# Modulation weights of a fused two-block transformer: eight buffers at the front, three in the heads, columns by transposes, and VectorE's weight splits placed later

## The reference

```python
s_lat = jax.nn.silu(c)[:, None, :]
s_ctx = jax.nn.silu(c_ctx)[None, None, :]
for i in range(DEPTH):                       # DEPTH = 2
    mod_l = jnp.split(s_lat @ ada_w[i] + ada_b[i], ADA_CHUNKS, axis=-1)   # ada_w[i]: 1024 x 6144
    mod_c = jnp.split(s_ctx @ ada_w[i] + ada_b[i], ADA_CHUNKS, axis=-1)
    h_lat = rms_norm(x_lat) * (1.0 + mod_l[1]) + mod_l[0]
    h_ctx = rms_norm(x_ctx) * (1.0 + mod_c[1]) + mod_c[0]
    ...                                      # retention_mixer(h_ctx, h_lat, w_in, ...) in layer 0
```

```python
proj = x @ w_in                              # qa ka va qb kb vb and the gates gl
ya = banded_attention(qa, ka, va) @ w_branch_a
yb = weighted(dilated_attention(qb, kb, vb) in 3 groups) @ w_branch_b
ga, gb = jnp.split(sigmoid(gl + b_gate), 2, axis=-1)
h = (ga * ya + gb * yb) @ w_out
```

## Time and profile before

| | us |
|---|---|
| median of 3 runs | 2275.52 |
| lowest, highest | 2269.53, 2278.43 |
| the profiled execution | 2268.73 |
| its span | 2266.9 |
| TensorE busy in it | 2112.4 (93%) |
| VectorE busy | 1129.0 (50%) |
| ScalarE busy | 877.7 (39%) |

### The profile page before, as it was taken

The page is one execution under the profiler, slowest core; times in us unless marked ns, Lnnn a source line. Parts: engine busy times, 40 slices in busy tenths (PEclk is TensorE's granted clock), DMA queues, the critical chain, the costliest instruction groups (busy, mean ns, idle before and its releaser), DMA issues.

```text
span 2266.9 us, 27438 instructions
## 1 busy us (share of the span) xinstructions
PE 2112.4 (93%) x11538; PEld 1762.1 (78%) x11538; DVE 1129.0 (50%) x1304; ACT 877.7 (39%) x1019; POOL 47.7 (2%) x75
## 2 busy tenths in 40 slices
PE   5799999999899999999988999998899999979998
PEld 3566676676777888877768998888799988878997
DVE  2314243242523243375666454766675567557555
ACT  3332232222322213245565443653454446434442
POOL 0000000000000000000000000000000000000000
PEclk9899999999999999999999999999999999999999
DMA  6634342535255333322134654553366545335552
GB/s 214 205 117 136 105 142 81 185 113 166 56 149 170 109 103 93 106 95 85 64 85 139 187 176 163 171 175 106 130 205 193 189 160 166 128 121 186 190 195 79
DMA packets 250637, 319.57 MB, mean 141 GB/s; under 512 B 9361, under 2 KB 165298, under 8 KB 250514
## 3 DMA queue, kind: packets, MB, share of 16 engines
q1 hardware_dynamic: 236050, 263.37, 36.2%
q0 software_dynamic: 14464, 54.45, 7.1%
HBM read 316.73 MB, written 1.05 MB: 140 GB/s over the span
## 4 chain that ended last, share of the span: by engine, by line
PE 74%; DVE 11%; DMA 5%; ACT 4%; DVEq 3%; issue 2%; ACTq 1%; POOL 0%; SPq 0%; POOLq 0%
PE ps L2126 22%; PE ps L2127 21%; PE ps L2128 21%; DMA raw<-ada_w 4%; DVE w_lo L1216 3%; PE ps L2143 3%; PE ps L2154 2%; PE ps L2234 2%; ACT w_hi L587 1%; DVE big_lo L1221 1%; PE ps L2289 1%; PE ps L2173 1%; DVEq L1233 1%; DVE hT_lo L1221 1%; ACT arena L834 1%
## 5 line engine op out<-in xcount | busy, mean ns | idle before, releaser
L1216 DVE TENSOR_TENSOR w_lo<-raw,w_hi 128x2048 fp32r<-128x2048 f32 (+1 forms) x244 | 553.2, 2273 | 480.7 <-ACT w_hi L587 480.1
L587 ACT ACTIVATE w_hi<-raw 128x2048 fp32r<-128x2048 f32 (+1 forms) x244 | 461.8, 1897 | 245.2 <-PE ps L2128 229.0
L2126 PE MATMUL ps<-h_hi,w_hi 128*128 128x256 f32 x1120 | 319.2, 285 | 2.9 <-DVE h_lo L1221 2.9
L2127 PE MATMUL ps<-h_lo,w_hi 128*128 128x256 f32 x1120 | 317.5, 283 | 0.0
L2128 PE MATMUL ps<-h_hi,w_lo 128*128 128x256 f32 x1120 | 317.4, 283 | 0.0
L2126 PE MATMUL ps<-w_hi,big_hi 128*128 128x512 f32 x760 | 302.3, 398 | 14.4 <-issue 10.2
L2127 PE MATMUL ps<-w_lo,big_hi 128*128 128x512 f32 x760 | 298.3, 392 | 0.0
L2128 PE MATMUL ps<-w_hi,big_lo 128*128 128x512 f32 x760 | 297.7, 392 | 0.0
L2126 PEld LDWEIGHTS ps<-h_hi,w_hi 128*128 128x128 f32 x1120 | 215.5, 192 | 6.1 <-issue 5.3
L2127 PEld LDWEIGHTS ps<-h_lo,w_hi 128*128 128x128 f32 x1120 | 215.6, 193 | 0.8 <-issue 0.2
L2128 PEld LDWEIGHTS ps<-h_hi,w_lo 128*128 128x128 f32 x1120 | 215.5, 192 | 0.0
(11 more groups left out here) (282 smaller groups left out, 2669.7 us busy)
## 6 DMA issues: line engine op xcount, KB each, us to landing
raw<-ffn_w_in SPq DMA_DIRECT2D x88, 512.0 KB, 5.1
raw<-ada_w POOLq DMA_DIRECT2D x40, 1024.0 KB, 5.6
raw<-w_in SPq DMA_DIRECT2D x80, 512.0 KB, 4.6
raw<-w_up SPq DMA_DIRECT2D x64, 512.0 KB, 4.8
raw<-w_down SPq DMA_DIRECT2D x64, 512.0 KB, 4.5
raw<-ret_w_in SPq DMA_DIRECT2D x48, 512.0 KB, 4.7
raw<-ffn_w_out SPq DMA_DIRECT2D x40, 512.0 KB, 4.5
raw<-diff_w_in SPq DMA_DIRECT2D x24, 512.0 KB, 4.6
```

Source lines behind the costliest of these rows:

```text
L587: act.activation(SPLIT_HI[PAIR_OF[u]][:, 0:m], raw[:, RAW_OF[u], 0:m], ACT.Copy).then_inc(sem["hi_ready"], 1)
L1216: op(SPLIT_LO[PAIR_OF[u]][:, 0:m], raw[:, RAW_OF[u], 0:m], SPLIT_HI[PAIR_OF[u]][:, 0:m].bitcast(F32), ALU.subtract).then_inc(sem["lo_ready ...
L2126: pe.matmul(out, a[0], b[0], start=start, stop=False)
L2127: pe.matmul(out, a[0], b[1], start=False, stop=False)
```

## The change

**Front.** The four chunks get eight half-chunk buffers `FRONT_IN`, laid over `big_hi` and `big_lo`, which are empty then. All units are split units now, `WHOLE` and its bookkeeping go, and the order on SP's queue becomes chunk 0, chunk 2, qa0, chunk 1, chunk 3, qb0. The six small vectors are issued by ScalarE instead of SP, x and ctx come first on POOL's queue and have a semaphore each. x is squared, scaled, turned (to `XTL`, in slot 0 of `raw`) and modulated apart from ctx, and strips qa0 and qb0 are done for the two x tiles first, then for the ctx tiles, with chunks between.

**Heads.** The halves 0 to 23 go round three buffers, two front buffers and slot 0; from 24 on slot 0 alone.

**Columns.** `to_cols` turns the four 128 x 128 blocks by transposes; VectorE adds the four partial sums with a reduction, then the bias.

**Layers.** In VectorE's stream four `ahead` calls move behind other work.

```diff
-    out = [("A0", 2, UNIT, True), ("A2", 2, UNIT, True), ("qa0", 1, UNIT, False)]
-    out += [("A1", 2, UNIT, True), ("A3", 2, UNIT, True), ("qb0", 1, UNIT, False)]
+    out = []
     for h in range(RH):
+        out += [(f"{n}{h}", UNIT) for n in ("qa", "qb", "g0", "g1", "va", "vb")]
...
-        r = u % 4 if u < 8 else 1 + (u - 8) % 3
+        r = 1 + u % 3
...
+        FRONT_IN = [sb(f"front{j}", [P, 4, 512], F32, big_at + 4 * UNIT * j)[:, :, :] for j in range(8)]
+        EXTRA_IN = [FRONT_IN[3], FRONT_IN[7], raw[:, 0, :].rearrange("p (k n) -> p k n", k=4)]
+        def extra_at(e):
+            return (e % 3, e // 3 + 1) if e < 24 else (2, e - 15)
...
# SP
             modulation(0)
+            modulation(1)
+            part(w, 0, 0, RH * RDK)
             modulation(2)
-            part(w, 0, 0, RH * RDK)
-            modulation(1)
             modulation(3)
             part(w, 4, 0, RH * RDK)
...
# POOL, modulation(e)
-                if e:
-                    pool.wait_ge(sem["ada_used"], e)
-                else:
-                    pool.wait_ge(sem["unit_used"], FIRST_END["qa0"])
-                fetch(raw[:, 0, :]..., kpn(A["ada_w"][d])[...], sem["ada_in"])
+                if e == 0:
+                    pool.wait_ge(sem["front_used"], 4)
+                if e == 2:
+                    pool.wait_ge(sem["xm_ready"], 4)
+                if e >= 3:
+                    pool.wait_ge(sem["ada_used"], e - 2 if e < 24 else e)
+                fetch(EXTRA_IN[extra_at(e)[0]], kpn(A["ada_w"][d])[...], ada_in[extra_at(e)[0]])
...
# ACT, the front
+            front(1)
             row(0, 8960, 0)
             turned_x(0)
+            front(2)
+            row(1, 9472, 1)
             turned_x(1)
+            act.drain()
+            act.wait_ge(sem["mod_ready"], 2)
+            modulate(0, 0, 1, 0, 0, lambda c: XTL[:, c, :])
+            split(FIRST_END["qa0"])
+            act.wait_ge(sem["xn_ready"], 2)
             turned_x(2)
             turned_x(3)
             act.drain()
+            modulate(0, 0, 1, 1, 0, lambda c: XTC[:, c, :])
+            split(FIRST_END["qb0"])
+            front(3)
             row(0, 8960, 2)
+            front(4)
             row(1, 9472, 3)
             act.wait_ge(sem["mod_ready"], 4)
+            modulate(0, 0, 1, 0, 4, lambda c: XTL[:, c, :])
+            modulate(0, 0, 1, 1, 4, lambda c: XTC[:, c, :])
...
# DVE, mod_cols
-                op(mod[:, d, 4 * n:4 * n + 4, :], bank(b)[:, 0:8].rearrange("p (j m) -> p j m", m=2), bias, ALU.add).then_inc(sem["mod_ready"], 1)
+                parts = bank(b).rearrange("p (j q m) -> p j m q", j=4, q=4)[:, :, 0:2, :]
+                m = mod[:, d, 4 * n:4 * n + 4, :]
+                dve.tensor_reduce(m, parts, AX.X, ALU.add)
+                drain()
+                op(m, m, bias, ALU.add).then_inc(sem["mod_ready"], 1)
...
# DVE, a layer of the second program
                 maxima_b()
+                normalise_b()
                 ahead("G4")
-                normalise_b()
                 ahead("G5")
...
                 maxima_b()
-                ahead("G7")
                 normalise_b()
                 pv_lo_b(1)
+                ahead("G7")
                 used("BA0")
...
                 branch_a(3, 21)
-                ahead("BA1")
                 ... (ple_hi: one subtraction)
                 pv_lo_b(2)
+                ahead("BA1")
                 pt_lo(5, 3)
                 pv_lo_b(3)
-                ahead("PL")
...
                 mix_lo(3)
+                ahead("PL")
                 ahead("BB")
...
# PE, to_cols
-                    i = pe.matmul(bank(b)[:, 2 * j:2 * j + 2], at(a, 512)[:, j * P:(j + 1) * P], select, start=True, stop=True)
+                    i = turn(bank(b)[:, j * P:(j + 1) * P], at(a, 512)[:, j * P:(j + 1) * P])
...
# PE, the front
+            strip(4, "qa0", hT, 0, 4, range(4), True, False, (0, 1))
+            chunk(2, 0)
             pe.wait_ge(sem["mod_ready"], 2)
             to_cols(2, 8960)
+            pe.wait_ge(sem["h_part"], 2)
+            strip(4, "qa0", hT, 0, 4, (0, 1), True, False, (2, 3))
+            chunk(3, 1)
+            strip(4, "qa0", hT, 0, 4, (2,), True, False, (2, 3))
             to_cols(3, 9472)
+            used(strip(4, "qa0", hT, 0, 4, (3,), True, False, (2, 3)))
+            pe.wait_ge(sem["h_part"], 3)
+            strip(4, "qb0", hT, 4, 4, range(4), False, True, (0, 1))
             pe.wait_ge(sem["h_part"], 4)
+            used(strip(4, "qb0", hT, 4, 4, range(4), False, True, (2, 3)))
```

More of the change, by code:

```diff
@@ L118 @@
 D0, U1 = FIRST_AT["q0a"], FIRST_AT["r0"]
-def unsplit():
-    out = [False] * TOTAL_UNITS
-    for name, n, _, whole in NAMED:
-        for u in range(FIRST_AT[name], FIRST_END[name]):
-            out[u] = whole
-    return out
-WHOLE = unsplit()
-SPLIT_UNITS = [u for u in range(TOTAL_UNITS) if not WHOLE[u]]
-SPLIT_NO = [sum(not w for w in WHOLE[:u]) for u in range(TOTAL_UNITS)]
-ORDER = [name for name, _, _, whole in NAMED if not whole]
 def slots():
@@ L181, in sizes @@
     out = [UNIT] * TOTAL_UNITS
-    for name, _, m, _ in NAMED:
-        out[FIRST_END[name] - 1] = m
+    for name, m in NAMED:
+        out[FIRST_AT[name]] = m
     return out
@@ L255, in build @@
         p_read = [sem["p_read0"], sem["p_read1"]]
-        unit_in = [ctx.enter_context(nc.semaphore(f"unit_in{r}")) for r in range(RAW_SLOTS)]
+        unit_in = {r: ctx.enter_context(nc.semaphore(f"unit_in{r}")) for r in range(1, RAW_SLOTS)}
+        front_in = [ctx.enter_context(nc.semaphore(f"front_in{j}")) for j in range(8)]
+        ada_in = [ctx.enter_context(nc.semaphore(f"ada_in{j}")) for j in range(3)]
         ident = const[:, C_IDENT:C_IDENT + P]
         dist = const[:, C_DIST:C_DIST + 384]
-        select = const[:, C_SEL:C_SEL + 2]
         def at(a, *dims):
@@ L366, in load @@
                 v = RAW_BEFORE[u]
-                if v is not None and WHOLE[v]:
-                    sp.wait_ge(sem["unit_used"], v + 1)
-                elif v is not None:
-                    sp.wait_ge(sem["lo_ready"], SPLIT_NO[v] + 1)
+                if v is not None:
+                    sp.wait_ge(sem["lo_ready"], v + 1)
                 for j in range(2):
@@ L593, in ahead @@
             def ahead(name):
-                split(SPLIT_UNITS[ORDER.index(name) + 2] + 1)
+                split(FIRST_END[name] + 2)
                 act.drain()
@@ L1308, in _ @@
             rows_split(0, 0)
+            split(FIRST_END["qa0"])
             rows_split(1, 0)
-            split(FIRST_END["qa0"])
+            split(FIRST_END["qb0"])
             mod_cols(2, 0, 1)
             mod_cols(3, 0, 3)
-            split(FIRST_END["qb0"])
             rows_split(0, 4)
@@ L2155, in sums, with chunk @@
                 return i
-            def chunk(name, b):
-                for j in range(2):
-                    u = FIRST_AT[name] + j
-                    pe.wait_ge(unit_in[RAW_OF[u]], 32 * RAW_FILL[u])
-                    used(sums(b, raw[:, RAW_OF[u], :].rearrange("p (k n) -> p k n", k=4), 4 * j))
+            def chunk(j, b):
+                for h in range(2):
+                    pe.wait_ge(front_in[2 * j + h], 32)
+                    i = sums(b, FRONT_IN[2 * j + h], 4 * h)
+                i.then_inc(sem["front_used"], 1)
             def extra(b):
                 e = s.next("extra") - 1
-                pe.wait_ge(sem["ada_in"], 16 * (e + 1))
-                sums(b, raw[:, 0, :].rearrange("p (k n) -> p k n", k=4), 4 * (e % 2)).then_inc(sem["ada_used"], 1)
+                r, n = extra_at(e)
+                pe.wait_ge(ada_in[r], 16 * n)
+                sums(b, EXTRA_IN[r], 4 * (e % 2)).then_inc(sem["ada_used"], 1)
             def to_cols(b, a):
```

157 lines of the change are left out of this document (71 added, 86 removed).

## The result

| | before | after |
|---|---|---|
| median us, same chip (4 runs each) | 2276.56 (2269.53 to 2278.43) | 2209.43 (2201.62 to 2218.7) |
| ratio of times | | 0.972, interval [0.970, 0.975] |
| the profiled execution, its span | 2268.7, 2266.9 | 2218.7, 2216.9 |

The change saves 67 us, 3%. The forecast was 2193; 2209 lies in its range, 16 us above it.

The account below looks back on a forecast made before the run. TensorE, busy 93% of the span, was taken to bound the kernel. Savings of 19 + 25 + 7 + 27 = 78 us from 2268.7 gave 2191, plus 2 for the median: 2193 us, own range 2176 to 2209.

Parts of the forecast that it names:

- Term 1: Front, to the end of strip qb0: without the slot limit 19 us saved, bounds 12 and 24.
- Term 2: Heads: three buffers remove the modulation-weight waits and the low clock behind the longest; 25 us saved, bounds 16 and 26.
- Term 3: Transposes instead of selector products in 20 places outside the front: 7 us saved, bounds 5 and 8.
- buffers do not help: Rival, heads: landings stretch or POOL's order holds one back, 25 us not gained; 2218 us, chance 0.09.
- Turns dear: Rival: four transposes apart from others may cost more than a quarter of 16 in a row; 2202 us, chance 0.03.
- Term 4: Two layers: VectorE's splits moved behind urgent work, 27 us saved, bounds 12 and 34.
- (d): Layers, gate mixes: without the split ahead of them the output strip starts earlier; 3.7 us saved, 1.4 of low clock.
- (a): Layers: softmax scaling before w_lo's subtraction frees 3.3 us, but the next softmax round follows only about 2.8 earlier.
- (b): Layers, at 1554.84 us: the same reordering of scaling before w_lo's subtraction, 2.6 us more.
- (c): Layers, turn at 1576.41: short subtractions first, turn 6.5 us earlier; with two of low clock, embedded values 8.5 earlier.
- given back in the layers: Rival: moved splits come late, TensorE waits for w_lo, only about 10 of 27 us stay; 2210 us, chance 0.16.

Follow-up runs that it names:

- e1: Changed kernel with POOL's queue issuing the decay and the lambdas ahead of x and ctx: 2207.79 us, 0.9719.
- e10: Changed kernel with small transfers first, values' splits ahead of G6, G7 and BA1 and of BA1's gates, x squared before lambda's exponential: 2186.63 us.
- e8: e1 with the fetch of ctx also waiting for chunk 0 to land: 2213.61 us, 0.9737.
- e3: Changed kernel with each modulation load of the heads waiting for the use of the one before it: 2239.74 us, 0.9858.
- e11: e10 with the selector products in place of the transposes: 2195.58 us, 0.967.
- e2: Changed kernel with VectorE's four splits in the layers put back where they stood: 2231.81 us, 0.9822.
- e4: Changed kernel with the selector products in place of the transposes: 2209.08 us, 0.9739.

## Why the prediction was nearly right, step by step

**Term 1, the front, 19 us: mis-sized, about 8 came.** Strip qb0 ends at 78.4 us, not at 65.5; the forecast itself named 72 as the mark of a wrong front. The slot limit did go, and nothing there waits for a buffer. The step that failed is "ScalarE is stuck until lam's exponential at 13.72": I carried this time over from a profile in which the decay and the lambdas had their own place on the wires. The change put x and ctx, 2 MB, ahead of them on POOL's queue, and the exponential came at 21.40. Everything behind it slid: the turn of x to 26.14 (18.5 forecast), strip qa0 to 42.10 (33), strip qb0 to 64.48 (52.6). I had taken off 1 us for small vectors that "now share the wires with x on ScalarE's queue", and not looked at what stands behind x on POOL's. e1 gave back 4 us of the 7.7; e10 put the squares where they don't wait for lambda, and 1.8 more came. e8 excludes ctx's share of the wires as the cause of the rest, whose origin stays open between the vectors' new queue and the weights beside them. The forecast's chain of durations was nearly right: from the turn of x to qa0 it gave 14.5 us, and 16.0 were needed; from there to qb0 19.6, and 22.4; for qb0 12.9, and 13.9. So of the 12.9 us by which the front ends late, 7.6 are the turn's and 5.3 such small excesses.

**Term 2, the weights in the heads, 25 us: right.** With term 3's part (13 of its groups by 0.35 us, 5) the forecast asks 30 in this stretch, 29 came; e3 alone gives 27 for the buffers, in the two parts foreseen: 18.1 us of waits, and low clock. The rival "buffers do not help" has fallen.

**Term 3, the turns, 7 us: right in kind, 9 measured** (e11; 9 also by the rows). Four transposes take 0.35 us to the next start, where the forecast had 0.44, so 0.46 us a place were saved and not 0.35. The page that spoke against it, the Trainium skill's "TensorE: Matmul & The Clock Gate", Part 4, with some 275 ns a transpose, gives the wrong sum for these: the row of e10 has 0.60 us for all four from the first start to the last end, and 16 back to back take 0.11 us each. "Turns dear" has fallen.

**Term 4, the layers, 27 us: mis-sized, 9.5 to 13.6 came in the profiles, 19 to 20 by e2's and e1's medians.** Without the clock 16 us came, where the forecast's waits alone (10.2 a layer) made 20. Point (d) came as counted: the 5.1 us of the earlier trace rows became 1.3. Points (a) and (b) came for the first and third turns, which wait no more (3.4 and 2.6 before). But the second turn's wait grew from 0.5 to 3.1 us, since G6's split (2.29 us) stood ahead of 0.4 us of urgent work, the very pattern that the change undoes elsewhere; I had looked only at the splits that it moves. In (c) 3.3 of 4.1 us stayed. The clock made the larger error in the profiles: I booked 3.4 us a layer as *saved* low clock, each beside a wait that would go. None can be shown to be saved. The profiled executions had 29 us of low time in the layers before and 44 after, since a stretch of 13.7 us stood behind the new wait in both layers; but other executions of the same order had 33, and e2, with the old order, 43. The low time of one profile is no property of the code that can be booked. The rival "given back in the layers" (2210) gave the time that came, but its mechanism (w_lo late at the third output unit and at the branches) is not in the profile: between 1460 and 1580 us no wait for w_lo is left, and the 2.2 us of such waits elsewhere in the first layer (1.1 us at most) stood there before as well.

**The level.** The forecast took the median before at 2275.5 and added 2 of 7 us to the profiled sum. Of the 16 us by which it missed, front and layers explain more (11 and 7 to 17); the heads and turns together are even. By the profiled executions alone the miss is 28 us (50 saved of 78), since the changed kernel was profiled in its slowest execution and the kernel before in its fastest; that the median lies within 16 us owes something to where the clock fell. The stated bounds of the terms (45 to 92 us saved) add up to 2179 to 2226 us, not to the 2176 to 2209 that the prediction names as its own range; the wider range of 2167 to 2223 holds the result either way.

## What to carry to other kernels

When a large transfer is moved ahead on a queue, list what stands behind it on that queue and who reads it first: here 4 KB, read 12 us later than before, held a whole chain. When splits are moved behind urgent work, do it for every such pair in the loop, since the next one becomes the wait; then compare the code's variants with the low clock counted apart: one and the same kernel varied by 17 us, and by 7 with the clock taken out. A verdict on a 9 us edit from one pair of runs had the wrong sign here (e4); the clock counted apart and a second base (e10 and e11) gave it right.

## What the runs showed of the hardware

A wait of 3.1 us was followed by 13.7, 3.4 or 0 us at half clock, and one of 3.4 us by 10.2, 3.4 or 0, with nothing different in the code of the layers; of the 13.7 us (1497.2 to 1510.9 in the changed kernel, granted clock 0.50) TensorE was busy for 12.5. On POOL's queue the 4 KB of the decay took 2.9 us to land as the first transfer, 5.3 with the weights started just beside it (e1), and 13.2 behind 2 MB. The six small vectors (80 KB together) were read at 6.7 us before, when they went ahead of the weights on SyncE's queue, at 8.9 after, by ScalarE's beside them, and at 10.7 to 11.1 with the decay and lambdas ahead of x.
